# S5 stage: states of blocks 0 and 1 moved ahead of later response jobs, their scans in the room of matrix C

## The chip, the core and the metric

The program runs on one core of one Trainium2 chip. The metric is device time in microseconds (us) of one execution, a median over several runs. TensorE is called PE below, VectorE DVE, ScalarE ACT, GpSimd POOL, and SyncE, whose queue issues the transfers here, SP.

## The reference, cut to what matters

The network is two transformer-like blocks on 512 tokens of width 1024. The last mixer of the second block is a state space layer (S5): 64 groups of 16 channels, each with 64 complex states. Only this layer is touched; it is written here in short form.

```python
def s5_mixer(h, w_in, log_dt, a_re, a_im, b_re, b_im, c_re, c_im, d_skip, w_glu, b_glu, w_out):
    u = h @ w_in                                     # 512 x 1024
    ab = exp((a_re + i a_im) * dt)                   # one complex factor per state
    bb = (ab - 1) / a * b                            # discretised input matrix
    bu = einsum('blgc,gpc->blgp', u, bb)
    x = associative_scan(x[t] = ab * x[t-1] + bu[t]) # 512 steps, 4096 complex states
    y = real(einsum('blgp,gcp->blgc', x, c)) + d_skip * u
    g = gelu(y)
    z = g * sigmoid(g @ w_glu + b_glu)
    return z @ w_out
```

## The kernel before

The kernel is a sequence of stages; each ends with a barrier of all engines. The change lies in `s5_stage`, which starts at 2096.4 us of the profiled execution and hands over to `glu_stage` at about 2198 us; its first product starts at 2200.3 us.

The 512 steps are cut into 64 chunks of 8. Within a chunk the outputs come from a table of impulse responses (`tab.k_t`), across chunks from the states at the chunk starts, which a scan of 64 steps gives. The 4096 states lie as 32 tiles of 128 partitions; a block b is 8 tiles, a job n of the responses is 8 tiles too, and there are four of each. PE works strictly in the order in which its calls are written:

- `responses(n)` (line 4370): products of the stored input powers `v` with matrix C, into banks 4 and 5. After every second one ACT copies a half into `kern` (line 4473). When both halves stand, DVE adds the skip term to `kern` (line 4613) and raises `k_final`; SP then stores `kern` to memory (line 4341) and loads it back in another layout with eight transfers (line 4348) into `tab.k_t`. All eight together raise `k_loaded`.
- `turn_b(n)` (line 4385): turns `v` of job n into the input matrices `tab.b_t`, in four groups over banks 0, 1, 6 and 7, each copied out by ACT (`copy_b`, line 4479).
- `turn_in(b)` (line 4397): turns the inputs of block b, through banks 0 and 1; ACT copies them into `ut[b % 3]` (`copy_in`, line 4492).
- `states(b)` (line 4409): the chunk inputs of the scan, into banks 2 and 3; DVE's `scan(b)` (lines 4557 to 4590) reads them and leaves the states in `x[b % 3]`. The scan uses the rooms `w`, `m` and `z`.
- `outputs(b)` (lines 4426 to 4432): needs `tab.k_t` whole (`k_loaded`, for b = 0), `ut` and `x`. Then come the GELU in pieces on ACT and DVE and `turn_out(b)` (line 4441).

Rooms are shared. `ut[0]`, `ut[1]`, `x[0]` and `x[1]` lie over the input powers of jobs 0 and 1, so `copy_in` waits for job 0's turns and `scan(0)` waits for `b_turned` 8 (both turns done) and for POOL's zeroes before it writes `x`. `x[2]` lies over `kern` and waits for the store. `ut[2]` lies in `resp.ut`, which holds matrix C until DVE has formed the last two quarters of the table `tab.c_t` (`resp.table`, lines 4297 to 4299, twelve operations at the head of DVE's queue in this stage). `z` lies in `resp.d_row`, which holds the skip term until line 4613 has read it: that is why DVE's first scan stands behind line 4613.

The queue of PE is `R0 R1 Tb0 R2 Ti0 R3 Ti1 S0 Tb1 S1 Tb2 Ti2 S2 Tb3 O0 Ti3 S3 O1 ...`, with R for responses, Tb and Ti for the two turns, S for states and O for outputs. The queue of DVE is: table, line 4613, scan(0), scan(1), scan(2), gelu(0), scan(3), and so on.

Of the kernel before, what the change touches and what calls it, by code (L numbers as in the profile page):

```python
# [4301 lines left out]
def s5_stage(k, tab, par, resp, u, g, g_parts, parts, raw):  # L4302
# [9 lines left out]
    TILES, CHUNKS = 8, S5_CHUNKS  # L4312
    B = J // TILES
    UTS, JOBS = 3, J // JQ
# [1 line left out]
    GELU = 2 * math.sqrt(2 / math.pi)  # L4316
    sides = S5_SIDES
    with k.stage("s5", "v_loaded", "turn_loaded", "zeroed", "k_done", "k_copied", "k_final", "k_stored", "k_loaded", "b_turned", "b_copied",
                 "c_formed", "x_zeroed", "u_turned", "u_copied", "s_done", "s_read", "vec_step", "x_ready", "y_done", "sq_done", "inner_done", "sig_done",
                 "g_ready", "o_turned", "copied", "raw_loaded", "next_high", "next_low", "g_high", "g_low") as (block, s, sb):  # L4320
        kern = sb("kern", [P, 2, J, GC])
        free = k.x[:].rearrange("p k t -> p (k t)")
# [1 line left out]
        flat_kern = kern[:].rearrange("p g j c -> p (g j c)")  # L4324
        x = [r.rearrange("p (r j t) -> p r j t", r=2, j=TILES) for r in
             [free[:, (2 + n) * TILES * P:(3 + n) * TILES * P] for n in range(2)] + [flat_kern]]
        w, m, z = (r.rearrange("p (r j t) -> p r j t", r=2, j=TILES)
                   for r in (par.b[:].rearrange("p r j c -> p (r j c)"), par.room[:], resp.d_row[:].rearrange("p r j c -> p (r j c)")))
        room = k.h.rearrange("p k t -> p (k t)")
        gt = room[:, 0:2 * TILES * P].rearrange("p (b e j c) -> p b e j c", b=2, j=TILES, c=GC)  # L4330
        q = room[:, 2 * TILES * P:2 * TILES * P + 3 * T].rearrange("p (n t) -> p n t", n=3)
# [30 lines left out]
        def _(pe):  # L4362
# [11 lines left out]
            def turn_b(n):  # L4374
                v = resp.v(n)
                for i in range(4):
                    r, h = i // 2, i % 2
                    if n >= 1:
                        pe.wait_ge(s["b_copied"], 4 * (n - 1) + i + 1)
                        if i < 2:  # L4380
                            pe.wait_ge(s["u_copied"], (4 if n == JOBS - 1 else 2) + i + 1)
                    for j in range(JQ):
                        for side in sides:
                            src = v[r][side, j, S5_HALF * h:S5_HALF * (h + 1), :].rearrange("p l c -> p (l c)")
                            mm = pe.matmul(ps[side, B_BANKS[i], j * STATE:(j + 1) * STATE], src, k.ident[side, side], start=True, stop=True)
                    mm.then_inc(s["b_turned"], 1)

            def turn_in(b):
                for n in range(2):
                    if b == 0:  # L4390
                        pe.wait_ge(s["b_copied"], n + 1)
                    else:
                        pe.wait_ge(s["u_copied"], 2 * (b - 1) + n + 1)
                        if b >= 2:
                            pe.wait_ge(s["b_copied"], 4 * b + n + 1)
                    for j in range(4):
                        mm = pe.transpose(ps[:, n, j * P:(j + 1) * P], u[:, TILES * b + 4 * n + j].rearrange("p g l c -> p (g l c)"), k.ident[:])
                    mm.then_inc(s["u_turned"], 1)
# [44 lines left out]
                        mm.then_inc(s["o_turned"], 1)  # L4443

            responses(0)
            responses(1)
            turn_b(0)
            responses(2)
            turn_in(0)
            responses(3)  # L4450
            turn_in(1)
            states(0)
            turn_b(1)
            states(1)
            turn_b(2)
            turn_in(2)
            states(2)
            turn_b(3)
# [11 lines left out]
        def _(act):  # L4470
# [11 lines left out]
            def copy_in(b):  # L4482
                for n in range(2):
                    act.wait_ge(s["u_turned"], 2 * b + n + 1)
                    if b == 0:
                        act.wait_ge(s["b_turned"], 4)
                        act.wait_ge(s["k_done"], 1)
                    if b >= UTS:
                        act.wait_ge(s["y_done"], 2 * (b - UTS + 1))
                    elif b == UTS - 1:  # L4490
                        act.wait_ge(s["c_formed"], 1)
                    act.activation(ut[b % UTS][:, 4 * n:4 * n + 4, :], ps[:, n, :].rearrange("p (j t) -> p j t", j=4), ACT.Copy).then_inc(s["u_copied"], 1)

            def squares(b):
# [21 lines left out]
                for c in of(b):  # L4516
                    act.activation(g_parts[:, 0, c], g[:, c, :], ACT.Copy).then_inc(s["g_high"], 1)

            responses(0)
            copy_b(0)  # L4520
            copy_in(0)
            responses(1)
            copy_in(1)
            copy_b(1)
            copy_b(2)
            copy_in(2)
            copy_b(3)
            for b in range(B):
# [18 lines left out]
        def _(dve):  # L4547
            step = Steps(dve, s["vec_step"])

            def scan(b):  # L4550
                mine = slice(TILES * b, TILES * (b + 1))
                c, sn = tab.turn[:, 0, mine, :], tab.turn[:, 1, mine, :]
                sr, si = (ps[:, 2 + r, :].rearrange("p (j t) -> p j t", j=TILES) for r in range(2))
                dve.wait_ge(s["s_done"], b + 1)
                if b >= 1:
# [52 lines left out]
                    dve.tensor_tensor(g_parts[:, 1, c], g[:, c, :], g_parts[:, 0, c].bitcast(F32), ALU.subtract).then_inc(s["g_low"], 1)  # L4608

            resp.table(step, dve, tab, range(2, 4))  # L4610
            dve.sem_inc(s["c_formed"], 1)
            dve.wait_ge(s["k_copied"], 2)
            dve.tensor_tensor(kern[S5_LAST], kern[S5_LAST], resp.d_row[S5_LAST], ALU.add).then_inc(s["k_final"], 1)
            dve.wait_ge(s["k_final"], 1)
            dve.wait_ge(s["turn_loaded"], 16)
            scan(0)
            scan(1)
            scan(2)
            for b in range(B):
                gelu(b)  # L4620
# [302 lines left out]
```

## Time and profile before

| | us |
|---|---|
| median of three runs | 2683.86 |
| lowest and highest of them | 2682.32 and 2688.01 |
| the profiled execution | 2686.32 |
| its span in the trace | 2684.6 |
| S5 stage, first product to first product of the next stage | 103.9 |
| of it, up to `outputs(0)` | 57.1 |

The time of an execution is 1.7 us more than the span, which starts with the first and ends with the last record. A clock of 1.00 in a window is TensorE at 2.4 GHz, 0.50 at 1.2 GHz, and values between are a mixture.

### The profile page before, as it was taken

The numbers are of one execution on the slowest core, as the hardware profiler recorded it, in microseconds if no ns is written. First come the engines' busy times: TensorE is split into PE (matmuls) and PEld (weight loads), VectorE is DVE, ScalarE is ACT, GpSimd is POOL, SyncE is SP. The second block draws the span as 40 slices with busy tenths as digits, with TensorE's granted clock in tenths as the row PEclk, the third lists the DMA queues.
The fourth block names the chain that finished last, engine by engine and source line by source line (L and its number), as shares of the span: only waits on it lengthen the run. The fifth ranks groups of instructions, "written<-read, shape, count | busy, mean of one in ns | idle before, by whom it ended". The sixth has DMA issues, their size and how long they took to land. (4 is left out here: it accounts for less than half of the span.)

```text
span 2684.6 us, 32750 instructions
## 1 busy us (share of the span) xinstructions
PE 2478.7 (92%) x12771; PEld 1954.2 (73%) x12771; DVE 1741.6 (65%) x2532; ACT 1139.3 (42%) x1641; POOL 46.6 (2%) x154
## 2 busy tenths in 40 slices
PE   7999899999989998799995898999998989899998
PEld 5666588677767876688872456788887877688886
DVE  6899545487775666899965565677765664642434
ACT  4544422255554224688863333622324244531323
POOL 0000001000000000100001000000000000000000
PEclk7999999999999997899996999999999889999998
DMA  6887727233324743899972113234331423223321
GB/s 229 280 274 266 263 81 279 76 104 85 94 85 170 255 96 141 322 421 419 417 279 95 59 44 102 63 121 145 111 110 58 144 75 124 70 95 101 101 81 32
DMA packets 299499, 427.39 MB, mean 159 GB/s; under 512 B 27690, under 2 KB 213533, under 8 KB 289488
## 3 DMA queue, kind: packets, MB, share of 16 engines
q1 hardware_dynamic: 291504, 395.40, 43.0%
q0 software_dynamic: 5392, 20.97, 2.0%
q10 hardware_dynamic: 2448, 8.91, 0.8%
q8 instruction: 102, 1.67, 0.3%
q14 instruction: 53, 0.43, 0.0%
HBM read 384.11 MB, written 41.14 MB: 158 GB/s over the span
## 5 line engine op out<-in xcount | busy, mean ns | idle before, releaser
L3715 PE MATMUL banks<-big,late_parts 128*128 128x512 f32 x1920 | 442.5, 392 | 11.1 <-DVE late_parts L3899 7.3
L3715 PEld LDWEIGHTS banks<-big,late_parts 128*128 128x128 f32 x1920 | 362.9, 189 | 89.2 <-DVE late_parts L3899 7.5
L3715 PE MATMUL banks<-h_parts_second,late_parts 128*128 128x512 f32 x1440 | 332.9, 392 | 12.8 <-DVE h_parts_second L3923 12.8
L3715 PEld LDWEIGHTS banks<-h_parts_second,late_parts 128*128 128x128 f32 x1440 | 272.3, 189 | 71.1 <-issue 14.4
L3899 DVE TENSOR_TENSOR late_parts<-w_second,late_parts 128x2048 fp32r<-128x2048 f32 x69 | 158.1, 2292 | 218.2 <-ACT late_parts L3784 218.0
L2377 DVE TENSOR_TENSOR expert_parts<-w,expert_parts 128x2048 fp32r<-128x2048 f32 x102 | 232.8, 2288 | 21.3 <-ACT expert_parts L2373 20.7
L3784 ACT ACTIVATE late_parts<-w_second 128x2048 fp32r<-128x2048 f32 x69 | 132.0, 1914 | 255.4 <-PE banks L3715 255.4
L1341 PE MATMUL banks<-h_parts,ssm_parts 128*128 128x512 f32 x960 | 232.4, 399 | 5.0 <-DVE ssm_parts L1610 4.3
L2373 ACT ACTIVATE expert_parts<-w 128x2048 fp32r<-128x2048 f32 x102 | 194.7, 1916 | 60.3 <-PE banks L2384 58.1
L1341 PEld LDWEIGHTS banks<-h_parts,ssm_parts 128*128 128x128 f32 x960 | 180.2, 190 | 51.1 <-issue 9.2
L2384 PE MATMUL banks<-expert_parts,expert_xt 128*128 128x512 f32 x816 | 193.4, 397 | 6.6 <-DVE expert_xt L2365 6.6
L2384 PEld LDWEIGHTS banks<-expert_parts,expert_xt 128*128 128x128 f32 x816 | 154.5, 191 | 39.4 <-DVE expert_xt L2365 7.4
L883 PE MATMUL banks<-h_parts,front_parts 128*128 128x512 f32 x552 | 137.9, 400 | 3.5 <-SPq L160 3.5
L553 PE MATMUL banks<-h_parts,front_parts 128*128 128x512 f32 x576 | 132.3, 391 | 2.7 <-PEq L151 2.7
L553 PEld LDWEIGHTS banks<-h_parts,front_parts 128*128 128x128 f32 x576 | 108.0, 188 | 26.4 <-issue 4.2
L3807 ACT ACTIVATE tail_r<-banks,cols 128x512 f32<-128x512 f32 x64 | 40.5, 685 | 202.5 <-PE banks L3715 202.5
L553 PE MATMUL banks<-h_parts,ssm_parts 128*128 128x512 f32 x480 | 114.2, 400 | 6.0 <-DVE h_parts L1964 3.1
L883 PEld LDWEIGHTS banks<-h_parts,front_parts 128*128 128x128 f32 x552 | 101.7, 190 | 23.8 <-SPq L160 3.9
L3932 DVE TENSOR_TENSOR tail_q<-tail_r 128x512 f32<-128x512 f32 x64 | 41.4, 688 | 115.4 <-ACT tail_r L3807 115.3
L1135 DVE SCALAR_TENSOR_TENSOR attention_mod_sum<-w,silu_c,attention_mod_sum 128x512 f32<-128x512 f32 x147 | 110.4, 751 | 5.4 <-DMA w<-in_mod_ffn_w_dram 1.0
L553 PEld LDWEIGHTS banks<-h_parts,ssm_parts 128*128 128x128 f32 x480 | 92.9, 194 | 26.9 <-issue 3.9
L2384 PE MATMUL banks<-expert_parts,expert_ht 128*128 128x512 f32 x408 | 98.6, 398 | 3.0 <-ACT experts_y L2871 3.0
(701 smaller groups left out, 3763.9 us busy)
## 6 DMA issues: line engine op xcount, KB each, us to landing
w_second<-in_mlp_w_dram SPq DMA_DIRECT2D x64, 1024.0 KB, 5.4
w<-in_w_exp_gate_dram SPq DMA_DIRECT2D x34, 1024.0 KB, 8.7
w<-in_w_exp_up_dram SPq DMA_DIRECT2D x34, 1024.0 KB, 8.5
w<-in_w_exp_down_dram SPq DMA_DIRECT2D x34, 1024.0 KB, 8.6
w<-in_w_in_dram SPq DMA_DIRECT2D x64, 512.0 KB, 4.7
w<-in_mod_mix_w_dram SPq DMA_DIRECT2D x24, 1024.0 KB, 5.0
w<-in_mod_ffn_w_dram SPq DMA_DIRECT2D x23, 1024.0 KB, 5.6
w<-in_w_in_dram SPq DMA_DIRECT2D x16, 1024.0 KB, 5.4
```

Of the source, the lines that this page charges most:

```text
L553: mm = pe.matmul(out, self.parts[:, n % 2, w, kk, f * P:(f + 1) * P], x[:, v, kk, :], start=(start and kk == 0 and j == 0), stop=(stop and ...
L883: mm = pe.matmul(ps[:, bank, :], parts[:, j, w, kk, :], k.hp[:, x, kk, :], start=(kk == 0 and n == 0), stop=(kk == KD - 1 and n == 2))
L1135: ins = dve.scalar_tensor_tensor(out=acc, in0=w, scalar=by, in1=acc, op0=ALU.mult, op1=ALU.add)
L1341: mm = pe.matmul(ps[:, t % 2, :], parts[:, t % SPLITS, w, kk, :], k.hp[:, x, kk, :], start=(kk == 0 and j == 0), stop=(kk == KD - 1 and j ...
L2373: act.activation(self.high_part(h), self.raw(h), ACT.Copy).then_inc(self.high_done, 1)
L2377: dve.tensor_tensor(self.low_part(h), self.raw(h), self.high_part(h).bitcast(F32), ALU.subtract).then_inc(self.low_done, 1)
L2384: mm = pe.matmul(out, x[:, v, first + kk, :], self.tile(h, w, kk), start=(start and kk == 0 and j == 0), stop=(stop and kk == KE - 1 and j ...
L3715: mm = pe.matmul(ps[:, bank(n, f), :], w_part(n, w)[:, kk, f * P:(f + 1) * P], x[:, v, kk, :], start=(first_chunk(n) and kk == 0 and j == ...
L3784: act.activation(w_part(n, 0), raw_half(k, n), ACT.Copy).then_inc(s["high_done"], 1)
L3807: act.activation(r[:, c % 2, :], ps[:, bank(n, c % HT), :], ACT.Relu, bias=k.cols[:, b1 + at:b1 + at + 1]).then_inc(s["relu_done"], 1)
L3899: dve.tensor_tensor(w_part(n, 1), raw_half(k, n), w_part(n, 0).bitcast(F32), ALU.subtract).then_inc(s["low_done"], 1)
L3932: dve.tensor_tensor(q[:, c % 2, :], r[:, c % 2, :], r[:, c % 2, :], ALU.mult).then_inc(s["squared"], 1)
```

## The change

PE's queue becomes `R0 Tb0 Ti0 S0 R1 Tb1 Ti1 S1 R2 R3 Tb2 Ti2 S2 Tb3 O0 ...`. ACT's copies follow the same order. DVE does scan(0) and scan(1) before line 4613. For that, the scans of blocks 0 and 1 use `resp.ut` (matrix C's room, free once the table is formed) in place of `resp.d_row` as their `z`. Since `ut[2]` lies in the same room, the copy of block 2's inputs waits for `x_ready` 2 (scan(1) done) in place of `c_formed`. The waits on banks 0 and 1 are renumbered for the new order. No operation is added or taken out but one semaphore increment.

```diff
-        w, m, z = (r.rearrange("p (r j t) -> p r j t", r=2, j=TILES)
-                   for r in (par.b[:].rearrange("p r j c -> p (r j c)"), par.room[:], resp.d_row[:].rearrange("p r j c -> p (r j c)")))
+        w, m, early, late = (r.rearrange("p (r j t) -> p r j t", r=2, j=TILES)
+                             for r in (par.b[:].rearrange("p r j c -> p (r j c)"), par.room[:], resp.ut[:].rearrange("p j t -> p (j t)"),
+                                       resp.d_row[:].rearrange("p r j c -> p (r j c)")))
...
                     if n >= 1:
                         pe.wait_ge(s["b_copied"], 4 * (n - 1) + i + 1)
                         if i < 2:
-                            pe.wait_ge(s["u_copied"], (4 if n == JOBS - 1 else 2) + i + 1)
+                            pe.wait_ge(s["u_copied"], 2 * (n - 1) + i + 1)
...
                     else:
                         pe.wait_ge(s["u_copied"], 2 * (b - 1) + n + 1)
-                        if b >= 2:
-                            pe.wait_ge(s["b_copied"], 4 * b + n + 1)
+                        pe.wait_ge(s["b_copied"], 4 * b + n + 1)
...
             responses(0)
+            turn_b(0)
+            turn_in(0)
+            states(0)
             responses(1)
-            turn_b(0)
+            turn_b(1)
+            turn_in(1)
+            states(1)
             responses(2)
-            turn_in(0)
             responses(3)
-            turn_in(1)
-            states(0)
-            turn_b(1)
-            states(1)
             turn_b(2)
...
                     elif b == UTS - 1:
-                        act.wait_ge(s["c_formed"], 1)
+                        act.wait_ge(s["x_ready"], 2)
...
-            responses(0)
             copy_b(0)
             copy_in(0)
+            responses(0)
+            copy_b(1)
+            copy_in(1)
             responses(1)
-            copy_in(1)
-            copy_b(1)
             copy_b(2)
...
+                z = early if b < 2 else late
...
             resp.table(step, dve, tab, range(2, 4))
-            dve.sem_inc(s["c_formed"], 1)
+            dve.wait_ge(s["turn_loaded"], 16)
+            scan(0)
+            scan(1)
             dve.wait_ge(s["k_copied"], 2)
             dve.tensor_tensor(kern[S5_LAST], kern[S5_LAST], resp.d_row[S5_LAST], ALU.add).then_inc(s["k_final"], 1)
             dve.wait_ge(s["k_final"], 1)
-            dve.wait_ge(s["turn_loaded"], 16)
-            scan(0)
-            scan(1)
             scan(2)
```

## Rows read from the trace of the kernel before

**Rows 1.** The page: span and share of each engine (busy us, share, instructions).
```profile
span 2684.6 us, 32750 instructions
...
PE 2478.7 (92%) x12771; PEld 1954.2 (73%) x12771; DVE 1741.6 (65%) x2532; ACT 1139.3 (42%) x1641; POOL 46.6 (2%) x154
```

**Rows 2.** Windows of the S5 stage: us, busy per engine, PEclk, DMA share, GB/s.
```profile
2096.40:2153.50 57.10, 52.04 (x1048) 51.03 (x1050) 38.56 (x47) 13.52 (x23) 3.68 (x4) 0.85 0.46 133
2153.50:2187.50 34.00, 33.26 (x678) 31.77 (x674) 28.58 (x44) 17.10 (x28) 0.00 (x0) 1.00 0.01 3
2187.50:2200.30 12.80, 1.97 (x9) 1.57 (x8) 7.71 (x13) 8.76 (x18) 0.00 (x0) 0.68 0.00 0
```

**Rows 3.** Timeline of PE: start, us, instructions, idle before and releaser.
```profile
2096.39 10.49 PE L4370 MATMUL banks<-late_parts_plain,x 128*128 128x32 f32 x64 [0.94 <-PEq L151]
2106.81 5.51 PE L4385 MATMUL banks<-ident,x 64*64 64x64 f32 x128
...
2116.75 3.66 PE L4370 MATMUL banks<-late_parts_plain,h_parts_second_plain 128*128 128x32 f32 x32
...
2126.59 3.89 PE L4385 MATMUL banks<-ident,x 64*64 64x64 f32 x128
2131.23 2.87 PE L4409 MATMUL banks<-x,big_plain 64*64 64x64 f32 x91 [0.75 <-issue]
2137.66 2.29 PE L4409 MATMUL banks<-x,big_plain 64*64 64x64 f32 x37 [3.57 <-issue]
...
2144.15 1.09 PE L4397 MATMUL banks<-ident,late_parts_plain 128*128 128x128 f32 x8
2145.99 3.95 PE L4409 MATMUL banks<-s_ut,big_plain 64*64 64x64 f32 x128 [0.74 <-ACT s_ut L4492]
...
2153.50 0.39 PE L4426 MATMUL banks<-big_plain,x 64*64 64x128 f32 x4
```

**Rows 4.** Timeline of DVE in the same stage.
```profile
2110.24 1.23 DVE L4299 TENSOR_TENSOR w_second<-w_second,s_room 128x1024 f32<-128x1024 f32 x1
2121.08 1.22 DVE L4613 TENSOR_TENSOR s_kern<-s_kern,s_d_row 32x1024 f32<-32x1024 f32 x1 [9.61 <-ACT s_kern L4473]
2126.90 0.69 DVE L4557 TENSOR_TENSOR s_b<-big_plain,banks 128x512 f32<-128x512 f32 x1 [4.60 <-PE banks L4409]
...
2132.76 0.65 DVE L4581 TENSOR_TENSOR x<-big_plain,s_d_row 128x504 f32<-128x504 f32 x1
...
2135.89 0.68 DVE L4590 TENSOR_TENSOR x<-x,s_room 128x504 f32<-128x504 f32 x1
```

**Rows 5.** Timeline of SP's queue in the stage: start and time to issue.
```profile
2097.21 0.43 SPq L4339 DMA_DIRECT2D big_plain<-s_rotations  x1
2122.33 0.32 SPq L4341 DMA_DIRECT2D s_kernels<-s_kern  x1
2124.90 4.71 SPq L4348 DMA_DIRECT2D big_plain<-s_kernels  x8
```

**Rows 6.** DMA issue of the rotations: KB, median us to landing.
```profile
big_plain<-s_rotations SPq DMA_DIRECT2D x1, 2048.0 KB, 11.6
```

**Rows 7.** Landing of the eight loads of line 4348.
```profile
DMA to landing us min/median/max: 4.7/6.9/9.4
```

**Rows 8.** Windows of 1 us: the granted clock at its changes.
```profile
2100.00:2101.00 1.00, 1.00 (x8) 1.00 (x7) 0.96 (x2) 0.00 (x0) 0.00 (x0) 0.53 0.92 393
2110.00:2111.00 1.00, 1.00 (x36) 1.00 (x34) 0.96 (x2) 0.49 (x1) 0.00 (x0) 0.85 0.00 0
2120.00:2121.00 1.00, 1.00 (x9) 1.00 (x9) 0.00 (x0) 0.55 (x1) 0.00 (x0) 0.77 0.00 0
2123.00:2124.00 1.00, 1.00 (x24) 1.00 (x24) 0.00 (x0) 0.00 (x0) 0.00 (x0) 0.52 0.89 369
2137.00:2138.00 1.00, 0.34 (x6) 0.34 (x8) 0.00 (x0) 0.00 (x0) 0.00 (x0) 0.80 1.09 310
2140.00:2141.00 1.00, 1.00 (x24) 1.00 (x22) 1.00 (x2) 0.00 (x0) 0.00 (x0) 0.50 0.04 14
```

More of the change, by code:

```diff
@@ L4318, in s5_stage @@
     with k.stage("s5", "v_loaded", "turn_loaded", "zeroed", "k_done", "k_copied", "k_final", "k_stored", "k_loaded", "b_turned", "b_copied",
-                 "c_formed", "x_zeroed", "u_turned", "u_copied", "s_done", "s_read", "vec_step", "x_ready", "y_done", "sq_done", "inner_done", "sig_done",
+                 "x_zeroed", "u_turned", "u_copied", "s_done", "s_read", "vec_step", "x_ready", "y_done", "sq_done", "inner_done", "sig_done",
                  "g_ready", "o_turned", "copied", "raw_loaded", "next_high", "next_low", "g_high", "g_low") as (block, s, sb):
```

## The prediction

> **What bounds the kernel now.** I read the page first. PE is busy for 92% of the span [rows 1], so a change that touches no product can pay only where PE stands still or waits in line. The change lies in one stage, so the next view is a table of stretches of that stage. It falls into three. Up to the first outputs there are 57.1 us with PE busy for 52.0 and a mean clock of 0.85. From there 34.0 us follow with 33.3 busy at clock 1.00. Then come 12.8 us of tail, in which PE does 2.0 us of work [rows 2]. The middle stretch is PE's own chain: whatever moves `outputs(0)` moves the end of the stage by as much, and the tail hangs on its last product. So I count one quantity: when `outputs(0)` can start, 2153.50 in the trace of before [rows 3].
>
> What sets that moment now is PE's own queue. The timeline of PE shows its pieces end to end, with a hole of 3.57 us in the middle of `states(1)`, and two holes of 0.75 and 0.74 us before `states`, where PE waits for ACT's copy [rows 3]. The other inputs of `outputs(0)` stand earlier. Line 4613 ends at 2122.3 and SP issues the store at 2122.33 [rows 4, 5]. The eight loads are issued from 2124.90 over 4.71 us [rows 5]. The last is issued at about 2129.2 and lands at most 9.4 us later, so `k_loaded` is complete at about 2138.6 [rows 5, 7]. That is 15 us of slack. From the end of line 4613 to the last landing are 2138.6 - 2122.3 = 16.3 us; this is the length that matters below.
>
> **The change, part by part.** No product, copy or scan goes away. Orders move, so I rebuild the queues from 2096.39 on with durations of before.
>
> The pieces at full clock: responses 3.7 (3.66), turn_b 3.9 (3.89), states 3.95. From the end of a turn_b to the start of states are 2145.99 - 2144.15 = 1.84: turn_in of 1.09 and the wait of 0.74 for ACT's copies [rows 3]. The first stretch of half clock begins at 2100.1 and ends at 2110.3 [rows 8]. In it products take about 1.8 times as long; the two first responses took 10.49 where two others take 7.4 [rows 3].
>
> PE up to scan(1)'s input. R0 runs before the drop: 3.7, to 2100.1. Tb0 follows inside the stretch of half clock; I give it what it took before, when it too was partly slow, 5.45 (5.51 less the overlap of two pieces), to 2105.55. Then 1.85 to S0, S0 3.95, R1 3.7, Tb1 3.9, 1.85, S1 3.95. The sum is 3.7 + 5.45 + 1.85 + 3.95 + 3.7 + 3.9 + 1.85 + 3.95 = 28.35, so S1 ends at 2124.75. Before, S1 ended at about 2139.95.
>
> DVE. The table ends at 2111.47 [rows 4]. S0 ends at 2111.35, so neither waits for the other. The rotations, which scan(0) also needs, were issued at 2097.21 and take 11.6 us: 2108.8, no wait [rows 5, 6]. scan(0) starts at 2111.5 in place of 2126.90. Its first part takes 2132.76 - 2126.90 = 5.9 us, to 2117.4. Now a new wait ends last: `b_turned` 8, at 2118.95, and POOL's zeroes 0.2 later. Behind it stands only the rest of the scan, 3.8 us [rows 4], to 2122.95, and scan(1) wouldn't start before S1 ends in any case, 1.8 us later. The wait is hidden; without that cover it would cost 1.75. scan(1) takes 2136.57 - 2126.90 = 9.67 from 2124.85, to 2134.5 [rows 4]. Only now does DVE come to line 4613, which has become the late one: 1.22 us [rows 4], to 2135.75, in place of 2122.3. Its other input, the copy of the second half of `kern`, follows R3. R2 and R3 run from 2124.75 to 2132.15, and the copy takes 0.65 more (R3 ended at 2120.41 before, and line 4613 started at 2121.08 [rows 3, 4]), 2132.8; with one stretch of half clock 2134.3. Either is covered by scan(1), the second barely.
>
> SP. The store and the eight loads keep their number and order, with the weight load of 1 MB behind them as before. With the 16.3 us of before they are complete at 2135.75 + 16.3 = 2152.05. Queued behind the loads is only that weight load, whose data ACT reads only after the squares of `outputs(2)`, so its lateness costs nothing.
>
> PE from there. Tb2 3.9 from 2132.15, 1.85, S2 3.95, Tb3 3.9: ready for `outputs(0)` at 2145.8, or 2147.3 with one slow stretch. The new wait of `copy_in(2)` for scan(1), 2134.5, is over when its input comes (2136.5), so it costs nothing; without that cover it would delay S2 and scan(2). scan(2) begins when S2 ends, 2141.9 to 2143.4, and ends by 2153.1, 6 us sooner than before. Nothing after it gets faster by that, since GELU(0) needs `outputs(0)`. The stall of 3.57 us inside `states(1)` no longer counts either: if it comes again behind the loads, it falls into Tb3, in front of a wait that is longer.
>
> So the queue of PE gets shorter by 6.2 to 7.7 us, but `outputs(0)` waits for `k_loaded`: 2152.05 in place of 2153.50, a gain of 1.45. The 16.3 us in it are a single observation; the loads run in 4.7 to 9.4 us each [rows 7], and I give the sum 1.5 us to both sides.
>
> The clock. PE now idles for about 5 us just before `outputs(0)`. Before, the idle of 3.57 us was followed by half clock from 2137.2 to 2141.0 [rows 8], of which PE had some 3.3 us to work in; 3.3 * (1 - 1/1.8) = 1.45 us lost. I expect the same loss at the head of `outputs(0)`, where the clock was 1.00 [rows 2]. The bounds are 0 (a stall leaves PE busy until shortly before) and 3 (two such stretches).
>
> From their first issue to the last landing the eight loads took 2138.6 - 2124.9 = 13.7 us [rows 5, 7]. The Trainium skill, DMA: Bandwidth & Descriptors, section "Anatomy of one DMA", gives a transfer as about 2.0 us plus its bytes by 436 GB/s. By this the eight loads (1664 KB) would be an estimated 6 us, the table would stand before PE asks for it, and the change would bring rival A; the trace, with 13.7 us, disagrees for these loads.
>
> Sum: -1.45 + 1.45 = 0. I put a little weight on the lower bound of the clock term, hence -0.2. The profiled execution, 2686.32, would become 2686.1. It lies 2.5 us above the median of the runs, inside their spread of 5.7. Against the median the forecast is 2683.7.
>
> **The rivals.**
>
> A. The gain arrives whole: `k_loaded` is not the last input, `outputs(0)` starts at 2145.8 to 2147.3, without an idle before it. This gives -7 us, 2676.9. For it: PE's pieces really become that much shorter. Against: it needs the chain from scan(1) over line 4613 to the last landing to be 5 to 6 us shorter than the same steps were before, and it has no part that the change shortens. Chance 0.06.
>
> B. The half clock costs more. Each further stretch of half clock before S1 ends delays scan(1), line 4613, the store and the loads one for one, by about 1.5 us. R1 stands alone between products, and the clock has fallen once after R3, at 2120.3, for 3.7 us [rows 8]. One more stretch turns the sum positive, two (and one in the tail) give +3, 2686.9. By over 0.2% slower it becomes from four. This is the rival on the slower side. Chance 0.16, a fifth of it over 0.2%.
>
> C. The change moves nothing but order: the loads land as reckoned and the clock term is small or the stall of 3.57 us appears in `outputs(0)` itself, since its instructions must come over the same transfer engines as the loads. The records name no releaser for that stall but "issue", and it ended when the burst of loads was nearly through [rows 3, 8]. In `outputs(0)` it would give +3.6 + 0, 2687.3. Chance 0.08. The Trainium skill, Runtime: NRT & Kernel Launch, section "Instruction fetch mechanics", calls such refills mostly hidden; by that rule this rival had no price.
>
> The forecast has the other 0.70.
>
> **How the numbers follow.** A measurement of this kernel tells about 0.2% (5.4 us) from no change. The forecast's own range is its bounds: -1.5 - 1.5 to +1.5 + 1.5, with the spread of a median of few runs (1.5) on top: 2679.5 to 2688. B and C at +3 and +3.6 lie in it; A and the far end of B lie outside. The range is 2679 to 2688.5. Faster by over 0.2%: A and a little of the forecast's edge, 0.08. Slower: the far end of B, a bit of C, and unknown shifts downstream, 0.08. Within: 0.84.
>
> **What would show it.** S0 at about 2107.4 and scan(0) at 2111.5 confirm the first part; a pause in scan(0) before line 4581 of about 1.7 us the new wait. Line 4613 at about 2134.5, directly behind scan(1), and SP's store right after it show the late chain. PE must be idle in front of line 4426 for some 5 us, ending with the last landing of line 4348, with a granted clock near 0.5 in the first 3 us of `outputs(0)`. Then 33 to 35 us to the last outputs as before. The prediction is wrong if PE has no idle there (A), if line 4613 starts after 2137 (B), or if the last landing and the start of line 4426 lie apart (C).

## The result and the profile after

The changed kernel takes 2688.45 us against 2682.66, each a median of 20 runs, with a ratio of 1.0022 (95% interval 1.0016 to 1.0028). It is slower by some 6 us, where 2683.7 and no change were forecast. The number itself lies 0.05 us inside the upper end of the forecast's range, 2679 to 2688.5, and that is luck: over 20 runs the kernel before has a median 1.2 us below the 2683.86 from which the forecast counted. The profiled execution of the changed kernel, 2685.61, is one of its fastest, and that of before, 2686.32, one of the slower ones. So its span is 2683.8 us, shorter than the 2684.6 of before; its stages ahead of S5 happened to take 7.3 us less (2089.05 in place of 2096.39 at the first product). The spans say nothing here, and the stage must be measured from its own first product.

The stage in three stretches, as in [rows 2]: us, busy time per engine, clock, DMA share, GB/s.

```profile
2089.05:2150.70 61.65, 54.00 (x1047) 52.64 (x1049) 44.72 (x55) 13.36 (x23) 3.76 (x4) 0.83 0.44 123
2150.70:2186.30 35.60, 34.86 (x679) 33.41 (x675) 22.66 (x35) 17.08 (x28) 0.00 (x0) 0.95 0.01 3
2186.30:2199.10 12.80, 2.02 (x9) 1.57 (x8) 7.76 (x13) 8.81 (x18) 0.00 (x0) 0.70 0.00 0
```

From first product to first product of the next stage are 2199.14 - 2089.05 = 110.09 us, against 103.96 (2200.35 - 2096.39). The 6.1 us more are about the loss of the timed runs. Up to `outputs(0)` there are 61.7 in place of 57.1, and 1.6 are lost behind it, where the clock is 0.95 in place of 1.00. The tail is unchanged to 0.1.

The timeline of PE, which answers to [rows 3]:

```profile
2089.05 3.83 PE L4371 MATMUL banks<-late_parts_plain,x 128*128 128x32 f32 x32 [0.94 <-PEq L151]
2092.80 5.36 PE L4386 MATMUL banks<-ident,x 64*64 64x64 f32 x128
...
2099.92 3.95 PE L4409 MATMUL banks<-x,big_plain 64*64 64x64 f32 x128 [0.74 <-ACT x L4492]
2103.80 3.76 PE L4371 MATMUL banks<-late_parts_plain,x 128*128 128x32 f32 x32
...
2117.08 11.37 PE L4371 MATMUL banks<-late_parts_plain,h_parts_second_plain 128*128 128x32 f32 x64
2128.39 6.25 PE L4386 MATMUL banks<-ident,h_parts_second_plain 64*64 64x64 f32 x128
...
2136.40 3.95 PE L4409 MATMUL banks<-s_ut,big_plain 64*64 64x64 f32 x128 [0.74 <-ACT s_ut L4492]
2140.19 2.49 PE L4386 MATMUL banks<-ident,h_parts_second_plain 64*64 64x64 f32 x78
2148.10 2.93 PE L4386 MATMUL banks<-ident,h_parts_second_plain 64*64 64x64 f32 x50 [5.43 <-issue]
2150.72 0.74 PE L4426 MATMUL banks<-big_plain,x 64*64 64x128 f32 x4
```

The two rows before the last hold the wait (two timeline rows of one job mean that PE stopped between them): 78 products of turn_b(3), then 5.43 us of nothing, then the other 50. The operation of line 4613, which adds the skip term, is line 4616 in this kernel, and line 4348 is 4349; in the kernels further on they shift by one or two lines. DVE, as in [rows 4]:

```profile
2104.16 0.69 DVE L4558 TENSOR_TENSOR s_b<-big_plain,banks 128x512 f32<-128x512 f32 x1
...
2111.73 0.68 DVE L4582 TENSOR_TENSOR x<-big_plain,s_ut 128x504 f32<-128x504 f32 x1 [1.63 <-POOL x L4358]
...
2117.20 0.69 DVE L4558 TENSOR_TENSOR s_b<-big_plain,banks 128x512 f32<-128x512 f32 x1 [1.63 <-PE banks L4409]
...
2129.12 1.22 DVE L4616 TENSOR_TENSOR s_kern<-s_kern,s_d_row 32x1024 f32<-32x1024 f32 x1 [2.25 <-ACT s_kern L4473]
2140.45 0.69 DVE L4558 TENSOR_TENSOR s_b<-big_plain,banks 128x512 f32<-128x512 f32 x1 [10.11 <-PE banks L4409]
```

SP's queue, as in [rows 5], and the landings of line 4349's loads, as in [rows 7]:

```profile
2130.37 0.32 SPq L4342 DMA_DIRECT2D s_kernels<-s_kern  x1
2132.95 3.88 SPq L4349 DMA_DIRECT2D big_plain<-s_kernels  x8
```

```profile
DMA to landing us min/median/max: 4.3/7.7/9.4
```

Windows of 1 us, as in [rows 8]; the third number from the end is the clock:

```profile
2119.00:2120.00 1.00, 1.00 (x11) 1.00 (x10) 1.00 (x3) 0.00 (x0) 0.00 (x0) 0.92 0.00 0
2120.00:2121.00 1.00, 1.00 (x6) 1.00 (x6) 1.00 (x3) 0.00 (x0) 0.00 (x0) 0.50 0.00 0
2132.00:2133.00 1.00, 1.00 (x24) 1.00 (x22) 0.00 (x0) 0.60 (x1) 0.02 (x1) 0.50 0.48 184
2134.00:2135.00 1.00, 1.00 (x26) 0.93 (x23) 0.00 (x0) 0.67 (x2) 0.00 (x0) 1.00 0.91 225
2147.00:2148.00 1.00, 0.00 (x0) 0.00 (x0) 1.00 (x2) 0.00 (x0) 0.00 (x0) 0.57 0.69 237
2153.00:2154.00 1.00, 1.00 (x14) 1.00 (x12) 0.00 (x0) 0.00 (x0) 0.00 (x0) 0.51 0.00 0
2154.00:2155.00 1.00, 1.00 (x26) 1.00 (x24) 0.00 (x0) 0.00 (x0) 0.00 (x0) 1.00 0.00 0
```

The first half went as reckoned: S0 starts at 10.87 us into the stage, scan(0) at 15.1, it pauses 1.63 for POOL's zeroes, and S1 ends at 28.1 where 28.35 was reckoned. Then R2 and R3 together take 11.3 us where 7.4 were reckoned, since the clock is at half from 2119.9 to 2133.5 (PE is busy all that time). Tb2 takes 6.2 in place of 3.9 for the same reason. Line 4613 starts at 40.1, behind R3's copy and no longer behind scan(1) (DVE idles 2.25 for it). The last load is issued at 2136.4 and lands 9.4 later, 56.8 into the stage. `outputs(0)` starts only at 61.7, directly behind turn_b(3), which was held up for 5.43 us and finished at half clock.

### The profile page after: what moved, and what is told of

Read it like the earlier page. It is cut to its first block and busy times, and to the rows that moved or that the text cites. A ratio compares the mean times of both kernels' runs of the same rounds, so it can differ in the third digit from the quotient of the medians.

```text
span 2683.8 us, 32750 instructions
## 1 busy us (share of the span) xinstructions
PE 2478.5 (92%) x12771; PEld 1957.1 (73%) x12771; DVE 1739.8 (65%) x2532; ACT 1140.7 (43%) x1641; POOL 48.1 (2%) x154
## 5 line engine op out<-in xcount | busy, mean ns | idle before, releaser
L2373 ACT ACTIVATE expert_parts<-w 128x2048 fp32r<-128x2048 f32 x102 | 194.9, 1918 | 60.2 <-PE banks L2384 57.7
```

What stands on the lines that cost most here:

```text
L2373: act.activation(self.high_part(h), self.raw(h), ACT.Copy).then_inc(self.high_done, 1)
```

## The experiments

All times in the table are counted in us from the stage's first product, in one profiled execution of each kernel: the start of line 4613, the last landing of the eight loads, the length from the end of line 4613 to it, the start of `outputs(0)` (O0), and the length of the stage. The ratio is that of timed runs (5 to 20 of each kernel) against the kernel before, with its 95% interval. The timed runs of one kernel spread over some 10 us, and each stage here is that of a single execution; by stage and by ratio the difference from before agrees within 3 us in eleven kernels and differs by 6 in e7_final_first. In e3 and e5 the loads are shorter, so their landing is left out. e11 was run once and has no ratio.

Three theories of the loss are tested, by these numbers. Theory 1: two response jobs side by side bring TensorE's clock to half. Theory 2: PE waits for its own instructions, which come late while the response table is loaded. Theory 3: line 4613 is late, and with it the table.

| kernel | 4613 | last landing | 4613's end to it | O0 | stage | ratio |
|---|---|---|---|---|---|---|
| before | 24.7 | 42.2 | 16.3 | 57.1 | 104.0 | 1 |
| changed | 40.1 | 56.8 | 15.5 | 61.7 | 110.1 | 1.0022 (1.0016 to 1.0028) |
| e1_apart | 42.1 | 61.8 | 18.5 | 61.9 | 110.3 | 1.0017 (1.0009 to 1.0026) |
| e2_late_weights | 40.0 | 57.7 | 16.5 | 61.0 | 108.2 | 1.0021 (1.0011 to 1.0030) |
| e3_short_loads | 40.0 | | | 55.7 | 102.6 | 0.9992 (0.9982 to 1.0001) |
| e4_before_adjacent | 28.4 | 48.3 | 18.8 | 62.4 | 109.3 | 1.0019 (1.0010 to 1.0027) |
| e5_before_short_loads | 24.7 | | | 52.1 | 99.0 | 0.9972 (0.9960 to 0.9984) |
| e6_before_late_weights | 24.7 | 40.4 | 14.5 | 55.8 | 102.7 | 0.9996 (0.9985 to 1.0008) |
| e7_final_first | 36.7 | 58.8 | 20.9 | 58.9 | 108.6 | 0.9994 (0.9982 to 1.0006) |
| e8_mixed | 31.0 | 48.8 | 16.6 | 53.6 | 100.4 | 0.9986 (0.9973 to 0.9999) |
| e9_mixed_scans_first | 45.7 | 65.0 | 18.0 | 65.1 | 113.6 | 1.0046 (1.0033 to 1.0060) |
| e10_mixed_late_weights | 31.0 | 45.8 | 13.6 | 52.6 | 99.4 | 0.9991 (0.9982 to 1.0000) |
| e11_shifted | 28.2 | 46.1 | 16.7 | 61.2 | 108.1 | |
| e12_between | 43.1 | 61.6 | 17.3 | 61.7 | 110.1 | 1.0026 (1.0014 to 1.0039) |

### e1_apart

```diff
             turn_in(1)
+            responses(2)
             states(1)
-            responses(2)
             responses(3)
```

> The changed kernel with responses(2) moved in front of states(1), so that it no longer stands next to responses(3). Lengths count from the stage's first product; before has 57.1 us to outputs(0) and 103.9 to the next stage's first product, the changed kernel 61.7 and 110.1. Theory 1 (two response jobs side by side make the granted clock fall to half and stay there): the half clock of 13.6 us from responses(3) into turn_b(2) shrinks to at most one stretch of 3.7 us; responses(3) ends near 35, states(2) near 44.5. Line 4613 follows scan(1) at about 41, the loads are complete near 58, outputs(0) at 58 to 59.5, the stage 106 to 107.5, so 3 to 4 us faster than the changed kernel. Theory 2 (the loss is the wait for instructions inside turn_b(3), while the response table is loaded): the half clock doesn't matter; the wait stays at about 5 us wherever the loads meet turn_b(3) and the stage stays at 109 to 110. Theory 3 (the late line 4613 alone): outputs(0) is tied to scan(1) and gets no earlier than 61.

The half clock behaved as theory 1 has it: R3 takes 3.7 us and Tb2 3.9, both at full clock. The time did not follow, 110.3 and a ratio of 1.0017. The timeline of PE shows why:

```profile
2142.45 3.89 PE L4386 MATMUL banks<-ident,h_parts_second_plain 64*64 64x64 f32 x128
2155.70 0.69 PE L4426 MATMUL banks<-big_plain,x 64*64 64x128 f32 x4 [9.35 <-issue]
```

turn_b(3) runs in one piece and `outputs(0)` comes 9.35 us after it. It starts at 61.9, when the last load lands. scan(1) starts at 32.4 in place of 28.1, since responses(2) and 1.5 us of half clock now stand in front of its input, and line 4613 follows directly behind it at 42.1. The chain from there took 18.5 us in place of 15.5. So with the other losses removed the response table is the gate, as theory 3 has it; that theory's bound, 61, holds too.

### e2_late_weights

```diff
             sp.wait_ge(s["k_done"], 4)
+            sp.wait_ge(s["y_done"], 2)
             sp.dma_start(raw, ...)
```

> The changed kernel; the 1 MB load of the next stage's weights waits for the first block of outputs, so it no longer runs beside and behind the eight loads of the response table. Theory 2 (PE waits for its own instructions, which come through the same transfer engines as these loads): the wait of 5.4 us inside turn_b(3) falls to 2 or 3 us, outputs(0) starts at 58.5 to 59.5 in place of 61.7, the stage is 107 to 108. Theory 1 (half clock alone): states(2) ends at 51.3 as before and the wait inside turn_b(3) doesn't change, stage 110. If the last landing of the eight loads (56.8) was the gate, outputs(0) moves only as far as that landing does.

The wait inside turn_b(3) went from 5.43 to 4.71 us, `outputs(0)` from 61.7 to 61.0, less than theory 2 wanted; the stage is 108.2, and the ratio doesn't differ from that of the changed kernel. The weight load behind the table's loads is a small part of the wait.

### e3_short_loads

```diff
-                    sp.dma_start(tab.k_t[at:at + GC, 0:C - l]..., src)
+                    sp.dma_start(tab.k_t[at:at + GC, 0:1]..., src[:, 0:1])
```

> The changed kernel, but each of the eight loads of the response table brings only its first row, so 0.5 MB in place of 1.66 MB arrive; the other rows of the table stay zero, and the outputs lack most of the response within a chunk. Theory 2: no wait inside turn_b(3) over 1 us; outputs(0) directly behind turn_b(3), at 55 to 56.5, stage 103 to 104.5. Theory 1: the half clock after responses(2) is as long as in the changed kernel (13.6 us), since no load causes it; states(2) ends at 51.3 all the same. Theory 3 (line 4613 late): line 4613 stays at 40.1, store and loads are complete before 50, no gate.

The loads still number eight, but each brings 32 KB, 0.26 MB together and not the 0.5 MB of the expectation. The result is as theory 2 has it. PE's timeline:

```profile
2137.90 3.95 PE L4409 MATMUL banks<-s_ut,big_plain 64*64 64x64 f32 x128 [0.74 <-ACT s_ut L4492]
2141.69 2.49 PE L4386 MATMUL banks<-ident,h_parts_second_plain 64*64 64x64 f32 x78
2144.83 1.67 PE L4386 MATMUL banks<-ident,h_parts_second_plain 64*64 64x64 f32 x50 [0.65 <-issue]
2146.28 0.44 PE L4426 MATMUL banks<-big_plain,x 64*64 64x128 f32 x4
```

After the same 78 products the wait is 0.65 us in place of 5.43, the clock stays at full, and `outputs(0)` follows at 55.7. The loads alone cost the changed kernel 110.1 - 102.6 = 7.5 us. R2 and R3 take 11.2 us here too: their half clock, from 30.9 to 44.6, doesn't depend on these loads, the first of which is issued at 43.8.

### e4_before_adjacent

```diff
             turn_b(0)
             responses(2)
-            turn_in(0)
             responses(3)
+            turn_in(0)
             turn_in(1)
```

> The kernel before, with only turn_in(0) moved behind responses(3), so that responses(2) and responses(3) stand side by side, and nothing else. Theory 1: the half clock from 2120.3 to 2124.0 comes sooner or lasts longer, by 3.4 to 7 us; the stage is 1.5 to 3 us longer than 103.9. Theory 2 or 3: no change beyond 0.5 us, as line 4613 even gets its input 0.3 us sooner.

Moving 1 us of transposes out from between two response jobs made the kernel before 1.0019 times as long. PE's timeline:

```profile
2110.99 9.56 PE L4370 MATMUL banks<-late_parts_plain,h_parts_second_plain 128*128 128x32 f32 x64
2120.37 3.75 PE L4397 MATMUL banks<-ident,late_parts_plain 128*128 128x128 f32 x16
2124.05 4.82 PE L4409 MATMUL banks<-x,big_plain 64*64 64x64 f32 x128
...
2139.15 1.90 PE L4409 MATMUL banks<-x,big_plain 64*64 64x64 f32 x37 [2.94 <-issue]
...
2146.91 1.38 PE L4385 MATMUL banks<-ident,h_parts_second_plain 64*64 64x64 f32 x38 [2.27 <-issue]
```

The two jobs take 9.4 us in place of 7.1, the turn_in jobs 3.7 in place of 2.5, and half clock lasts 10.3 us in place of 3.4. Line 4613 gets 3.7 us later. Then the waits for instructions are 2.94 and 2.27 where before had one of 3.57. The stage is 109.3, 5.3 longer, more than the 1.5 to 3 of theory 1: 3.4 of it come from the clock, and most of the rest is the longer waiting (5.2 us in place of 3.6).

The other traces agree. responses(2) and (3) stand side by side in four kernels (changed, e2, e3, e4), and there the half clock lasts 10.3 to 13.7 us; in the ten others it lasts up to 3.5 us near these jobs, and 6.9 and 6.8 in e10 and e12.

### e5_before_short_loads

The edit of e3_short_loads in the kernel before; the loads bring 0.26 MB here too.

> The kernel before, with the eight loads of the response table cut to their first row (0.5 MB in place of 1.66 MB; the other rows stay zero, so the outputs lack most of the response within a chunk). Theory 2 (instructions held up by the loads): the wait of 3.57 us inside states(1) and the half clock after it vanish, outputs(0) at 51.5 to 52.5 in place of 57.1, stage 98.5 to 99.5 in place of 103.9. Beside the changed kernel with the same cut (102.6) this gives what the new order costs without the loads: 3 to 4 us, by its longer half clock and three more waits for ACT's copies. Theory 3 (only the late table costs): the stage of before keeps its 103.9, as the table was never late there.

The stage is 99.0: the loads cost the kernel before 5.0 us, all in the wait and the half clock after it. The difference between the two orders without loads is 102.6 - 99.0 = 3.6 us. From the starts of the pieces in both: responses 18.5 against 17.5, turn_b 20.1 against 17.3, the rest 17.0 against 17.4. So the new order costs 3.6 us by itself, and 7.5 - 5.0 = 2.5 more come from where it puts the loads.

### e6_before_late_weights

The edit of e2_late_weights in the kernel before.

> The kernel before; the 1 MB weight load waits for the first block of outputs. Theory 2: the wait inside states(1) falls from 3.6 to 2.5 to 3 us, as it did by 0.7 in the changed kernel, the stage is 0.5 to 1.5 us shorter than 103.9. If the weight load is what holds the instructions up, the wait goes under 1 us and the stage to 100.

The wait is 2.25 us, a little less than theory 2 had; the stage is 1.3 shorter, inside its range; the ratio of 0.9996 can't tell that from nothing.

### e7_final_first

```diff
+                z = early if b < 1 else late
...
             scan(0)
-            scan(1)
             dve.wait_ge(s["k_copied"], 2)
             dve.tensor_tensor(kern[S5_LAST], ...).then_inc(s["k_final"], 1)
             dve.wait_ge(s["k_final"], 1)
+            scan(1)
             scan(2)
```

with PE's order of e1_apart, and `copy_in(2)` waits for `x_ready` 1.

> As e1_apart, and line 4613 stands in front of scan(1), which then uses the old room again (only scan(0) uses matrix C's). Theory 3 (in e1_apart the loads of the table end last, behind scan(1) and line 4613): line 4613 moves from 42.1 to 36.7, the last landing and with it outputs(0) from 61.9 to 56 to 57, the stage from 110.3 to 104 to 105.5. Theory 2: the loads now run while turn_b(3) does, so a wait for instructions of 3 to 5 us comes back inside turn_b(3), but it ends at or before the last landing, and the stage is the same 104 to 105.5. If neither holds, outputs(0) stays near 61.

The skip-term operation moved to 36.7 as expected, but the stage of 108.6 missed the expected 104 to 105.5: in the profiled execution the chain behind it took 20.9 us, the store 4.5 until the loads could be issued and the loads up to 13.2. `outputs(0)` again starts with the last landing, at 58.9. The timed runs say 0.9994, about 6 us better than e1_apart by the ratios, and the intervals lie apart. So by the timed runs, putting line 4613 in front of scan(1) gives back what e1_apart had lost against before; the one stage in the trace doesn't show it. Whether the chain is shorter in the other executions isn't known; the profiled one is as a whole only 0.5 us above the kernel's median.

### e8_mixed

PE's order is `R0 Tb0 Ti0 R1 S0 R2 Tb1 R3 Ti1 S1 Tb2 Ti2 S2 Tb3 O0`, DVE's that of e7_final_first. ACT's copies follow PE's order, and `copy_in(2)` waits for `x_ready` 1.

> PE's order is R0 Tb0 Ti0 R1 S0 R2 Tb1 R3 Ti1 S1 Tb2 Ti2 S2 Tb3 O0: no two response jobs side by side, all four done early, and responses in the place of two waits for ACT's copies. DVE does scan(0), line 4613, scan(1), with matrix C's room for scan(0) only. Theory 1: half clock before outputs(0) falls from 17.7 us (before) to two or three stretches of 3.4 to 3.7. Line 4613 at about 30, the table complete at 47.5, in front of PE's need. Theory 2: one wait of 3 to 5 us for instructions while the loads run. outputs(0) at 52 to 55, the stage 98.5 to 102, so 2 to 5 us faster than before (ratio 0.998 to 0.9995). If the half clock doesn't depend on the responses standing side by side, it is as long as before and the stage is 103 to 105.

This version beats the kernel before, by the narrowest margin in the timed runs, 0.9986 (0.9973 to 0.9999), and by 3.5 us in the stage, 100.4. It beats the changed kernel clearly. Up to `outputs(0)` no stretch of half clock lasts over 4 us:

```profile
2121.33 3.76 PE L4371 MATMUL banks<-late_parts_plain,h_parts_second_plain 128*128 128x32 f32 x32
...
2126.75 3.95 PE L4409 MATMUL banks<-x,big_plain 64*64 64x64 f32 x128 [0.76 <-ACT x L4492]
...
2136.20 2.54 PE L4409 MATMUL banks<-s_ut,big_plain 64*64 64x64 f32 x79 [0.74 <-ACT s_ut L4492]
2141.69 1.98 PE L4409 MATMUL banks<-s_ut,big_plain 64*64 64x64 f32 x49 [2.95 <-issue]
...
2148.42 0.39 PE L4426 MATMUL banks<-big_plain,x 64*64 64x128 f32 x4
```

The wait for instructions is still there, 2.95 us in states(2), and `outputs(0)` at 53.6 has 4.9 us of slack to the last landing at 48.8.

### e9_mixed_scans_first

PE's order of e8_mixed with DVE's order of the changed kernel.

> PE's order of e8_mixed (no response jobs side by side, all four done early), with DVE's order of the changed kernel: scan(0), scan(1), then line 4613. Theory 3 (standing behind scan(1) makes the response table the last input of outputs(0)): states(1) ends at 36, scan(1) at 45.6, line 4613 follows at 45.7 in place of 31.0, the loads are complete at 61 to 64 and outputs(0) starts with the last of them; half clock follows the idle; stage 109 to 112, ratio 1.002 to 1.003. If the table isn't a gate, the stage stays near 100.4.

```profile
2142.43 6.00 PE L4409 MATMUL banks<-s_ut,big_plain 64*64 64x64 f32 x128 [6.19 <-ACT s_ut L4492]
...
2151.50 1.67 PE L4386 MATMUL banks<-ident,h_parts_second_plain 64*64 64x64 f32 x50 [0.74 <-issue]
2160.57 0.69 PE L4426 MATMUL banks<-big_plain,x 64*64 64x128 f32 x4 [7.40 <-issue]
```

113.6, slightly beyond the range of theory 3, and 1.0046. The same PE order, with only scan(1) in front of line 4613, goes from 100.4 to 113.6. PE waits 6.19 us for block 2's inputs, whose copy waits for scan(1), and 7.40 for the last landing.

### e10_mixed_late_weights

The edit of e2_late_weights in e8_mixed.

> e8_mixed with the 1 MB weight load behind the first block of outputs. Theory 2: the wait for instructions in states(2) falls from 2.95 to 1.5 to 2.5 us, as in e6_before_late_weights (3.57 to 2.25); with it the stage goes from 100.4 to 99 to 100, ratio near 0.998. If the loads of the table alone set that wait, no change.

The wait in states(2) is gone, and one of 0.75 us stands in turn_b(2), one block sooner; the expectation had 1.5 to 2.5. The stage is 99.4, but half clock came for 7 us around states(1), where e8_mixed, with the same order of PE, has none. The ratio of 0.9991 is no better than that of e8_mixed; the intervals overlap.

### e11_shifted

```diff
-                    for j in range(4):
+                    for j in [j for j in range(4) for _ in range(5 if b == 0 else 1)]:
                         mm = pe.transpose(...)
```

> The kernel before with each transpose of turn_in(0) made five times, which adds 32 products (some 4 us) and changes nothing else. Counted in records of PE from the stage's first product, the wait of before comes after the 619th record, and the changed kernel's after the 998th, three times 128 less 5 further on. Theory 2 (it is PE's own instructions, fetched in blocks, that come late): the wait again falls on the 619th record or a multiple of 128 from it, so 32 records sooner inside states(1), after its 59th record in place of the 91st. If PE waits there for data or for a bank, the wait stays after the 91st record of states(1).

```profile
2134.36 1.93 PE L4409 MATMUL banks<-x,big_plain 64*64 64x64 f32 x59 [0.74 <-issue]
2139.34 2.97 PE L4409 MATMUL banks<-x,big_plain 64*64 64x64 f32 x69 [3.05 <-issue]
2142.00 2.83 PE L4385 MATMUL banks<-ident,h_parts_second_plain 64*64 64x64 f32 x58
2145.62 2.31 PE L4385 MATMUL banks<-ident,h_parts_second_plain 64*64 64x64 f32 x70 [0.80 <-issue]
```

With 32 records more ahead of it the wait comes after the 59th product of states(1), not the 91st of [rows 3], and the next, of 0.80, comes 127 records on. It is tied to a position in PE's stream of instructions and not to any data. In all kernels these waits come at four places, after record 619, 745 or 746, 871 and 998 of the stage.

The traces also hold the transfers of the instructions, as a DMA queue of their own. Each is one packet of 16 KB. In the changed kernel record 871 is passed at 2138.7, and the next packet starts only in the second of these windows (queue, packets, MB, share of the 16 engines):

2139.00 to 2145.50:

```profile
q1 hardware_dynamic: 753, 1.12, 107.4%
```

2145.50 to 2147.00:

```profile
q1 hardware_dynamic: 530, 0.54, 103.0%
q8 instruction: 1, 0.02, 4.2%
```

The packet runs from 2145.6 to 2146.6, 6.9 us after the record, and PE goes on at 2148.10. In the kernel before it starts 5.5 us after record 492, and with the short loads of e5_before_short_loads 0.3 us after the same record, without a wait; in e3_short_loads it starts 2.4 us after record 871. In all 13 waits of this kind, in eleven kernels, PE goes on 1.2 to 1.8 us after the end of such a packet. In e1_apart and e12_between the packet that record 998 needs starts at 46.0 and 47.3 us of the stage, within 0.4 us of the first load's issue, and there is no wait. So it is PE's instructions that come late: their packet starts late while the loads keep the transfer engines at a share of 107%, and on time or nearly so when the loads are short or not yet under way.

### e12_between

```diff
             states(1)
             responses(2)
-            responses(3)
             turn_b(2)
+            responses(3)
             turn_in(2)
```

and ACT's copies in the same order.

> The changed kernel with turn_b(2) between responses(2) and responses(3), and ACT's copies in the same order; DVE's order is untouched, so states(1) and scan(1) end when they did. Theory 1 with 2 (two response jobs side by side took away the cover, and the wait for instructions then came out in full): responses(3) ends near 39.5, line 4613 stays at 40, states(2) ends near 45 in place of 51.3, turn_b(3) is begun before the burst of loads; the wait for instructions is hidden in front of the last landing, outputs(0) starts with that landing at 57 to 60 (the loads' own spread), with half clock after an idle; stage 105 to 108, between before (103.95) and the changed kernel (110.1). Theory 2 alone: the wait inside turn_b(3) stays 5 us and the stage 109 to 110. Theory 1 alone: the stage gets 6 us shorter, 104.

```profile
2126.24 4.44 PE L4371 MATMUL banks<-late_parts_plain,h_parts_second_plain 128*128 128x32 f32 x32
2130.61 6.35 PE L4386 MATMUL banks<-ident,h_parts_second_plain 64*64 64x64 f32 x128
2136.89 3.76 PE L4371 MATMUL banks<-late_parts_plain,h_parts_second_plain 128*128 128x32 f32 x32
...
2146.10 3.90 PE L4386 MATMUL banks<-ident,h_parts_second_plain 64*64 64x64 f32 x128
2159.94 0.69 PE L4426 MATMUL banks<-big_plain,x 64*64 64x128 f32 x4 [9.95 <-issue]
```

The expectation of 105 to 108 missed. Half clock came at 2129 all the same and lasted 7 us, so R3 ended at 42.3, line 4613 started at 43.1 and the last load landed at 61.6. The wait for instructions is gone and turn_b(3) is done at 51.8, 9.9 us before it is of any use. `outputs(0)` starts where it did in the changed kernel, now by the other gate.

## Why the prediction was wrong

**What held.** The mechanism of its first half: the new wait in scan(0) is hidden, S1 ends within 0.3 us of the reckoning, line 4613 and the loads become late, nothing is gained by the earlier scans, and half clock lies over the head of `outputs(0)`, where 1.6 us were lost for the 1.45 reckoned. That last agreement is in part luck: the idle in front of the half clock was the wait inside Tb3, and not the reckoned one for the landing. Of the signs that the prediction named, two came true: PE has no idle directly in front of line 4426, though rival A didn't come with it, and the last landing and the start of line 4426 lie 4.9 us apart.

**First failed term: R2 and R3 at 7.4 us, with one stretch of half clock at most.** They took 11.3, and Tb2 6.2 in place of 3.9, together 6.2 us. The prediction allowed 1.5, and took the single fall of the clock behind R3 in [rows 8] as the whole risk. Its own rows held the warning: R0 and R1 side by side took 10.49 us, at half clock from 2100.1 to 2110.3 [rows 3, 8]. The change parts this pair, and half clock there shrinks to 3.4 us, which the prediction counted as a gain; it makes a new pair of R2 and R3, which the prediction counted at full clock. Its rival B put the half clock in front of S1, where it didn't come; rival A, the whole gain, had no part in what happened. e4_before_adjacent shows the cause in the kernel before: two response jobs side by side, and the clock falls during them and stays down some 10 us. e1_apart and e8_mixed, with something else between them, have stretches of 3.4. e12_between shows the rule is not exact, with one response job behind states(1) and 7 us of half clock, and e10_mixed_late_weights has 7 us in the same order in which e8_mixed has none there.

**Second failed term: "if it comes again behind the loads, it falls into Tb3, in front of a wait that is longer".** The wait for instructions came in Tb3, as said, but it was 5.43 us and the wait behind it was no longer there. With S2 late by 5.8 us, Tb3 would have ended at 55.2 without it, only 1.6 before the last landing (56.8). The wait and the half clock that followed it in Tb3 put the start at 61.7, 4.9 beyond the landing. e3_short_loads removed both with the loads. That it is PE's instructions that come late is shown by e11_shifted, where the place moves with the count of records, and by the instruction packets themselves; the wait of before comes after 619 records of the stage, that of the changed kernel after 998, which is 379 or close to three times 127 further on. Rival C had the mechanism and put it in `outputs(0)`, at +3.6; its chance was 0.08. This second term explains the profiled execution. It isn't the whole of the timed loss: e1_apart and e12_between have no such wait, their loads land at 61.8 and 61.6, and their ratios, 1.0017 and 1.0026, are no better than the changed kernel's.

**Third: the length from line 4613 to the last landing, 16.3 us, 1.5 to both sides.** In the changed kernel's profile it is 15.5. The last landing stood within 1.1 us of the reckoning, since line 4613 was 2 us late (it waited for R3's copy and not for scan(1)) and the chain 0.8 short. But over the nine kernels of the table in which the whole loads and the weight load follow each other it is 15.5 to 20.9. The timed runs of the changed kernel reach from 2685.6 to 2693.7, and part of this chain is now exposed in them; how often the landing and how often the wait for instructions decides is not known, since there is one trace of it.

**The sizes.** By e3 and e5 the order costs 3.6 us without the full loads (half clock, and the wait of 0.65), and the place of the loads 2.5 more; that is the 6.1 of the profile. Two readings of the prediction are slightly off: the windows of [rows 8] put the second and third stretch of half clock at 2120.5 and 2137.6, each 3.4 us long, and not at 2120.3 and 2137.2; this moves its sum by less than 0.3. What the two gates share is the late line 4613. In the pair e8_mixed and e9_mixed_scans_first the scan in front of it, with the copy that waits for that scan, is worth 13.1 us of the stage.

**Still open.** Why the same loads take 15.5 us in one execution and 20.9 in another, and when exactly one response job alone makes the clock fall.

The Trainium skill, Runtime: NRT & Kernel Launch, section "Instruction fetch mechanics", says that instructions are fetched in blocks of 256 and that this is mostly hidden. A product and its weight load are two instructions, so 128 records are a block, which fits the spacing of 127 between two waits in e4_before_adjacent and e11_shifted and the packets of 16 KB. That it is hidden does not hold in this stage: waits of up to 5.4 us stand open where a block is due during the burst of loads.

The other figure that the prediction took from the Trainium skill, 2.0 us plus the bytes by 436 GB/s (DMA: Bandwidth & Descriptors, "Anatomy of one DMA"), is given in that section for transfers that GpSimd issues. These eight loads come from SP's queue and took 13.7 and 12.9 us from first issue to last landing, and don't test that figure.

## What to carry to other kernels

Work that moves ahead of something in one engine's queue makes something else late: follow the release behind it (here store, loads, table) to its reader, and count its slack before and after. A duration read from a trace in which it had slack has a spread that the trace doesn't show, and once it becomes the gate that spread is in the time. Two gaps that would be hidden one behind the other can be hidden only once: when a first term grows, ask which cover it uses up.

## What the runs showed of the hardware

- With response jobs (weights of 128 by 128, moving 32 columns) side by side TensorE's granted clock went from 2.4 to 1.2 GHz although PE was busy all the time: for 10.3 us in e4_before_adjacent, 13.7 in the changed kernel. With another job between them the stretches were 3.4 to 7 us.
- PE's instructions come in packets of 16 KB on a DMA queue of their own, about one for every 127 products of 64 by 64 with their weight loads. While eight loads of together 1.66 MB, or the weight load behind them, ran, such a packet started up to 6.9 us after the record one block ahead of its use (0.3 and 2.4 us with loads of 0.26 MB, in e5 and e3), and PE stood for up to 5.4 us; it went on 1.2 to 1.8 us after the packet's end in all 13 waits. The wait was 2.3 to 5.4 us in eight kernels, 0.65 to 0.8 in e3, e9, e10 and a second one of e11, and none in e5, nor in e1_apart and e12_between, where the packet was ahead of the loads. The 1 MB weight load behind the loads is worth 0.7 us of it in the changed kernel and 1.3 in the kernel before.
- The eight loads, at a DMA share of 1.0 or over, moved 153 to 188 GB/s in the kernel before and the changed one and took up to 9.4 us each to land. In e7_final_first they moved 123 to 152 GB/s and took up to 13.2, with nothing changed about them.
